# Computing the w_mod product in four column groups of TensorE, from a buffer ring of its own, inside the delta rule

## The reference, cut to what matters

```python
# first block (D_MODEL 1024, SEQ 256)
h = h + gated_deltanet(rmsnorm(h, a_norm), ...)        # qkv, z, chunked delta rule, w_out
h = h + conv_ffn(rmsnorm(h, f_norm[0]), ...)           # up, conv, silu*val, down
kv = rmsnorm(h, kv_norm) @ w_kv
h = h + chunk_attention(rmsnorm(h, b_norm), ...)       # 16 heads, band of 576 keys
h = h + conv_ffn(rmsnorm(h, f_norm[1]), ...)
# second block
mod   = silu(c)     @ w_mod + b_mod                    # 1024 -> 6144, one row
mod_c = silu(c_ctx) @ w_mod + b_mod                    # and one for the context
sh1, sc1, g1, sh2, sc2, g2 = split(mod, 6)
hc = rmsnorm(ctx, norm1) * (1 + csc1) + csh1           # context rows
h  = rmsnorm(x, norm1)   * (1 + sc1)  + sh1
x  = x + g1 * (concat(retention, attention)(h @ w_in, hc @ w_in) @ w_out)
x  = x + g2 * (square(relu((rmsnorm(x, norm2) * (1 + sc2) + sh2) @ w_ff1)) @ w_ff2)
out = rmsnorm(x, final_norm)
```

## Time and profile before

| | before |
|---|---|
| device time, 3 runs | 1300.94, 1303.83, 1306.04 us (median 1303.83) |
| profiled execution: first to last instruction (span) | 1310.7 us |
| profiled execution: mean granted TensorE clock | 0.958 |
| PE busy | 1216.3 us (93% of the span) |
| PEld busy | 1065.0 us (81%) |
| DVE busy | 803.3 us (61%) |
| ACT busy | 567.6 us (43%) |
| POOL busy | 28.4 us (2%) |
| chain that ended last | PE 69%, issue 16%, DVE 9%, ACT 4%, DMA 2% |
| moved by DMA | 192.51 MB, 147 GB/s |

### The profile page before, as it was taken

The page is one execution under the profiler, slowest core; times in us unless marked ns, Lnnn a source line. Parts: engine busy times, 40 slices in busy tenths (PEclk is TensorE's granted clock), DMA queues, the critical chain, the costliest instruction groups (busy, mean ns, idle before and its releaser), DMA issues.

```text
span 1310.7 us, 22039 instructions
## 1 busy us (share of the span) xinstructions
PE 1216.3 (93%) x8276; PEld 1065.0 (81%) x8276; DVE 803.3 (61%) x1352; ACT 567.6 (43%) x918; POOL 28.4 (2%) x27
## 2 busy tenths in 40 slices
PE   4999999999999999898799999999999688999995
PEld 4997769847899988796578999885999456999884
DVE  4994565454588875444446888754456866455654
ACT  5554410023455454445445545544435445344552
POOL 0001000000000000000010000000100000000000
PEclk9997989899999999999799999999999899899998
DMA  7662420054666566555174566665433106466661
GB/s 200 161 187 71 153 72 1 17 177 138 192 185 189 179 208 194 150 176 173 49 257 129 173 179 192 206 194 178 129 97 97 33 1 198 117 184 191 204 194 51
DMA packets 226688, 192.51 MB, mean 147 GB/s; under 512 B 6784, under 2 KB 202496, under 8 KB 226368
## 3 DMA queue, kind: packets, MB, share of 16 engines
q1 hardware_dynamic: 223984, 184.67, 47.2%
q0 software_dynamic: 1456, 6.82, 1.4%
q10 hardware_dynamic: 1184, 0.14, 0.1%
HBM read 190.56 MB, written 1.05 MB: 146 GB/s over the span
## 4 chain that ended last, share of the span: by engine, by line
PE 69%; issue 16%; DVE 9%; ACT 4%; DMA 2%; POOL 1%; SPq 0%; DVEq 0%; POOLq 0%; ACTq 0%
PE ps L565 18%; PE ps L567 17%; PE ps L566 17%; PE ps L443 4%; PE ps L766 3%; PE ps L764 2%; DVE wL L1551 2%; PE ps L774 1%; PE ps L660 1%; DMA raw<-in_w_mod 1%; DMA raw<-in_a_w_in 1%; DVE st_p L1956 1%; ACT xH L1147 1%; ACT wH L1057 1%; PE ps L836 1%
## 5 line engine op out<-in xcount | busy, mean ns | idle before, releaser
L1551 DVE TENSOR_TENSOR wL<-raw,wH 128x1024 fp32r<-128x1024 f32 x298 | 354.7, 1222 | 185.4 <-ACT wH L1057 184.4
L565 PE MATMUL ps<-xH,wH 128*128 128x256 f32 x1216 | 348.2, 286 | 0.0
L566 PE MATMUL ps<-xL,wH 128*128 128x256 f32 x1216 | 347.3, 286 | 0.0
L567 PE MATMUL ps<-xH,wL 128*128 128x256 f32 x1216 | 347.1, 285 | 0.0
L1057 ACT ACTIVATE wH<-raw 128x1024 fp32r<-128x1024 f32 x298 | 302.1, 1053 | 95.1 <-PE ps L567 93.7
L565 PEld LDWEIGHTS ps<-xH,wH 128*128 128x128 f32 x1216 | 236.8, 195 | 2.3 <-issue 2.1
L566 PEld LDWEIGHTS ps<-xL,wH 128*128 128x128 f32 x1216 | 236.8, 195 | 0.0
L567 PEld LDWEIGHTS ps<-xH,wL 128*128 128x128 f32 x1216 | 236.7, 195 | 0.0
L565 PE MATMUL ps<-wH,xH 128*128 128x256 f32 x496 | 144.1, 291 | 3.7 <-DVE xL L1551 3.7
L1095 ACT ACTIVATE stage<-ps 128x512 f32<-128x512 f32 x84 | 50.2, 597 | 222.4 <-PE ps L567 222.4
L566 PE MATMUL ps<-wL,xH 128*128 128x256 f32 x496 | 142.7, 288 | 0.0
(11 more groups left out here) (333 smaller groups left out, 1444.4 us busy)
## 6 DMA issues: line engine op xcount, KB each, us to landing
raw<-in_f_w_up SPq DMA_DIRECT2D x88, 512.0 KB, 4.7
raw<-in_w_ff SPq DMA_DIRECT2D x64, 512.0 KB, 4.2
raw<-in_w_mod SPq DMA_DIRECT2D x48, 512.0 KB, 4.2
raw<-in_f_w_down SPq DMA_DIRECT2D x44, 512.0 KB, 4.3
raw<-in_a_w_in SPq DMA_DIRECT2D x32, 512.0 KB, 4.7
raw<-in_w_in SPq DMA_DIRECT2D x22, 512.0 KB, 4.6
raw<-in_w_kv SPq DMA_DIRECT2D x16, 512.0 KB, 4.6
raw<-in_a_w_out SPq DMA_DIRECT2D x8, 512.0 KB, 4.5
```

The costliest lines, as they stand in the source:

```text
L565: mm(o, l[0], r[0], start=first, stop=False, skip_group_check=check)
L566: mm(o, l[0], r[1], start=False, stop=False, skip_group_check=check)
L567: return mm(o, l[1], r[0], start=False, stop=last, skip_group_check=check)
L1551: return tt(o, x, hi.bitcast(F32), ALU.subtract)
```

## The change

The product runs with another shape and other buffers, and most of it at another place.

**Shape.** `cact` is now 32 columns wide, its columns 2 to 31 zeroed by POOL. A unit is four matmuls of 32 stationary and 256 moving columns, one for each row half k and column half x, and each writes to its own 32 PSUM partitions, 32 * (2k + x). So they lie in four column groups of the PE array. The two row halves are no longer summed by PSUM; the finish does it. `mrow` is 128 x 256, and the finish multiplies it by selection constants: `sel` (four matmuls against 2 columns, L454 of the changed kernel) or `selb` (two matmuls of 256 columns, L458). The constants grow by 260 columns of fp32 for each partition.

**Ring.** The units have a ring of three buffers, `modw`, loaded by POOL's queue in program order between POOL's inverse roots. The `raw` ring on SP carries only layer weights again.

**Place.** Forty units, ten chunks, are in the front of the delta rule and the delta rule itself: 8 among the z blocks, 8 among `products`, 16 in the doubling (the dictionary `fill`: 1 or 2 units after a step, -1 for a finish), 8 in the scan. One chunk stays around the norm f0 and one around kv. None is left in the band attention or around f1, n1 and n2.

```diff
-MOD_PLACES = (("wo_a", 5), ("up0", 1), ("k", 1), ("wo_b", 1), ("up1", 1), ("win", 2), ("ff1", 1))
+MOD_CHUNKS = 12
+MOD_RAW = 3
+MOD_AFTER = {"up0": 11, "k": 12}
-        cact = sb("cact", [P, KD, 2])
-        mrow = sb("mrow", [2, 2, 512])
+        cact = sb("cact", [P, KD, 32])
+        mrow = sb("mrow", [P, 2, 256])
+            modw = sb("modw", [P, MOD_RAW, 2, 512], where=s)
 # ModulationSteps.units
-                    self.pe.wait_ge(mod_in[self.m % RAW], 16 * (self.m // RAW + 1))
+                    self.pe.wait_ge(mod_in[self.m % MOD_RAW], 16 * (self.m // MOD_RAW + 1))
                     for k in range(2):
-                        last = nc.tensor.matmul(mod_bank(h)[0:2, :], cact[:, 2 * u + k],
-                                                raw[:, (U(name) + self.m) % RAW, k * 512:(k + 1) * 512],
-                                                start=u == 0 and k == 0, stop=u == 3 and k == 1)
+                        for x in range(2):
+                            q = 32 * (2 * k + x)
+                            last = nc.tensor.matmul(mod_bank(h)[q:q + 32, 0:256], cact[:, 2 * u + k],
+                                                    modw[:, self.m % MOD_RAW, k, x * 256:(x + 1) * 256],
+                                                    start=u == 0, stop=u == 3)
 # ModulationSteps.finish
-                        last = nc.tensor.matmul(mod_bank(h)[:, 2 * k:2 * k + 2], mrow[:, h % 2, k * P:(k + 1) * P],
-                                                ident[0:2, 0:2], start=True, stop=True)
+                        last = nc.tensor.matmul(mod_bank(h)[:, 2 * k:2 * k + 2], mrow[:, h % 2, (k % 2) * P:(k % 2 + 1) * P],
+                                                K_["sel"][:, 2 * (k // 2):2 * (k // 2) + 2], start=True, stop=True)
 # delta_front_pe
                 sums()
                 z(0)
+                mod.units(3)
                 square_sums()
...
                 z(1)
+                mod.units(1)
...
                 z(2)
+                mod.units(2)
...
                 z(3)
+                mod.units(2)
 # delta_pe
-                mod.units(4)
+                mod.finish()
+                mod.finish()
...
                 products(0)
+                mod.units(2)
                 for g in range(1, 4):
                     products(g)
                     turn_m(g - 1)
+                    mod.units(2)
                 turn_m(3)
-                mod.units(4)
+                fill = {(0, 0): -1, (0, 1): -1, (0, 2): 1, (1, 0): 1, (1, 1): 1, (1, 2): 1, (2, 0): 1, (2, 1): 1, (2, 2): 1,
+                        (3, 0): 1, (3, 1): -1, (3, 2): -1, (4, 0): 2, (4, 1): 2, (4, 2): 2, (5, 0): 2}
...
+                        if fill.get((l, step), 0) < 0:
+                            mod.finish()
+                        mod.units(max(fill.get((l, step), 0), 0))
...
                 heads(4, lambda n: AT[:, 8 + n], lambda n: P_[:, 8 + n])
-                mod.units(4)
                 mod.finish()
                 mod.finish()
-                mod.units(4)
 # band_pe
                 scores(0)
                 scores(1)
-                mod.units(4)
-                mod.finish()
 # program of PE
             token_major("wo_b", X)
-            mod.units(3)
             turn_rows("f1")
-            mod.units(1)
-            mod.finish()
...
-            mod.units(7)
             turn_rows("n1")
-            mod.units(1)
-            mod.finish()
-            mod.finish()
...
-            mod.units(3)
             turn_rows("n2")
-            mod.units(1)
-            mod.finish()
 # POOL
+            def mod_load(first, end):
+                for m in range(first, end):
+                    if m >= MOD_RAW:
+                        pool.wait_ge(mod_used, m - MOD_RAW + 1)
+                    ...
+                    pool.dma_start(modw[:, m % MOD_RAW], src).then_inc(mod_in[m % MOD_RAW], 16)
             norm("a")
+            pool.wait_ge(unit_done, 12)
+            mod_load(0, 6)
...
+            mod_load(6, 42)
...
+            mod_load(42, 43)
             norm("f0")
+            mod_load(43, 47)
...
             norm("kv")
+            mod_load(47, 48)
```

More of the change, by code:

```diff
@@ L331, in build @@
         cond_ready = sem("cond_ready")
-        mod_in = [sem(f"mod_in{i}") for i in range(RAW)]
+        mod_in = [sem(f"mod_in{i}") for i in range(MOD_RAW)]
         mod_used = sem("mod_used")
@@ L989, in _ @@
             pe.wait_ge(y_ready, 4)
-            pe.wait_ge(mod_act, sum(MOD_AT["wo_a"]))
+            pe.wait_ge(mod_act, 10)
             token_major("wo_a", X)
@@ L1244, in delta_act @@
                     cp(MT[:, 4 * g:4 * g + 4].rearrange("p a b -> p (a b)"), ps[2 + g % 2][:]).then_inc(mt_act, 1)
-                mod_keep()
-                mod_keep()
+                for _ in range(3):
+                    mod_keep()
+                    mod_keep()
+                    mod_place()
+                    mod_place()
                 def banks(first, bank, o):
```

108 lines of the change are left out of this document (38 added, 70 removed).

## The result

The changed kernel takes 1318.81 us (median; 1316.76 to 1320.81), the kernel before 1302.38 on the same chip: ratio 1.0133, 95% interval 1.0103 to 1.0162. So 16 us slower, where 3 us faster was forecast, and outside the range of 1288 to 1316.

What follows compares the result with a forecast made beforehand. The prediction took PE (93% busy) as the bound, but only where the stage waits for it. Its terms summed to -3.2 us, 1307.5 against the profiled span 1310.7, corrected to 1301 for the timed runs; range 1288 to 1316.

Steps and rivals of the forecast that it cites:

- The term for the larger constants: Before the first matmul: 0.13 MB of constants at 222 GB/s takes 0.6 us, counted as +0.5.
- the doubling's term: Doubling in the delta rule: 16 units 9.3 us, four finishes 4.2, +13.5; wrong above 20 or below 8.
- the base: Whole kernel: sum -3.2 on the profiled span 1310.7, then about 7 us off because timed runs lie lower.
- The price of a unit: Each unit of the product: 0.43 us with four column groups together, 0.86 at half clock; 1.81 before.
- The charge for entering: Entering and leaving the four-group form: 0.2 us a call (0 to 0.5).
- C: Only two column groups stream at once: unit 0.9 us, 30 units on the path, +12, 1313; chance 0.13.
- E: Groups run one after another: unit stays at 1.8 us, +42 less some 8, about 1335; chance 0.05.
- D: The ring starves: at 7 us a load +15, 1316; decides from about 5.5 us a load; chance 0.10.
- The front: Delta rule's front: units ahead of the column sums and among the z blocks, total +4.0 us (1 to 6).
- The set-up: Ahead of the doubling: eight units between products and turns, -4.8 us if hidden, 0 if not; half taken, -2.4.
- Scan and tail: Delta rule's scan +0.4 us together; tail, colder PE at y's transposes and first wo_a tiles, +1.2 (0 to 3).
- The norms: First matmuls of the layers behind the norms: f0 -2.8 us, kv +0.6, f1 -4.6, n1 -1.0, n2 -3.6.

Runs made afterwards that it cites:

- warm_setup: after_aligned plus four fp32 matmuls of 2 by 512 columns, result unread, in PE's gap ahead of the doubling; 1304.0 us, ratio 1.0027.
- before, second: The kernel before, profiled again with no edit; ratio 1.0001, span 1302.8 us.
- after_aligned: The changed kernel with 32 bytes of padding behind the constants, aH back at its old address; 1307.69 us, ratio 1.0049.
- after_x: The changed kernel with 32 bytes of padding ahead of xH and no other padding; 1297.37 us, ratio 0.9953.
- warm_tail: after_aligned plus sixteen fp32 matmuls of 2 by 512 columns, result unread, under DVE's closing work of the delta rule; 1304.47 us, ratio 1.0020.
- late8: after_aligned with the doubling's last eight units moved to the scan, the scan's eight under DVE's closing work with extra warming matmuls; 1303.97 us, ratio 1.0008.
- place_only: The changed kernel with the old unit shape (2 columns by 512) and the constants, cact and mrow of the kernel before; 1356.02 us, ratio 1.0397.
- finish_early: after_aligned with the finishes of chunks 2 and 3 ahead of the doubling's first step; 1302.18 us, ratio 1.0011.
- no_fill: The changed kernel without chunks 4 to 7: their 16 doubling units, loads, two finishes in the doubling and two in the scan; 1298.68 us, ratio 0.9976.
- spread: after_aligned with 12 of the doubling's 16 units moved: into the scan, under DVE's closing work, one chunk into the band attention; 1298.08 us, ratio 0.9980.
- shape_x: The kernel before with only the unit's shape changed, plus 32 bytes of padding ahead of xH; 1278.25 us, ratio 0.9821.

## Why the prediction was wrong

Two steps failed. The term for the larger constants, +0.5, held their DMA alone and put what they do to the addresses behind them at nothing, without a reason; that was 11 us, 6 of them countable. And the doubling's term, +13.5, had the units and the finishes but no clock; the doubling grew by 21.7, beyond the 20 from which the forecast had called itself wrong. A third error was in the base, and hid in the choice of the profile. The terms one by one:

**The price of a unit** was right: 0.43 for the second of a pair, and 0.57 alone with 0.17 more in the step behind it, 0.74 in all, against a forecast of 0.43 and 0.2. In the timeline four records of a unit start within 0.02 us and the other four 0.22 to 0.24 us later. An estimate from the speedup for three column tiles that the Trainium skill gives (TensorE: Matmul & The Clock Gate, Measured speedup vs the span model) would be 0.55; the trace has four groups at 0.43. The charge for entering, which the Trainium skill's rule on draining (TensorEngine Tiling (Array Packing), Key Properties) had put in doubt, is 0.14 for the unit and 0.17 for the step behind it, and the second of these the old shape pays as well. Rivals C and E are out, and D too: the loads took 4.5 us in the median, below the 5.5 from which D decides.

**The front** was sized wrongly by 4 us in the change's favour. I had priced three units at half clock. They ran at full clock, 1.50 us in all, and the 64 column sums behind them took 10.23 instead of 13.67 (13.58 in the earlier trace rows), because the clock fell at 109 us and not at 102. The forecast had taken 1 us off for this and not 3.4.

**The set-up** came out at -1.1 instead of -2.4: the doubling starts 6.9 earlier and the finishes 0.1 later, which makes -7.0, of which the finishes are 1.68 - 7.55 = -5.9. The ring of three was the brake, as written: two loads, of 4.28 and 5.41 us, stand in the chain there.

**The doubling** is the step that failed in the delta rule: +21.7 against +13.5. Its own terms add up to 8 x 0.74 + 5.1 for the four pairs + 3.5 for the finishes = 14.5, near the 13.5. The other 7 are the clock: 6.27 - 3.77 for the first step, which starts cold, and 2.9 + 0.4 + 1.6 for the second fall. I had written that the old units ahead of the doubling cost 9.25 us and could go. They had also done their slow first half at low clock while DVE was not ready yet, and the doubling then ran from its start at a clock of 1.00. I read that clock and didn't ask what had brought it about. With four matmuls for nobody in that gap (warm_setup) the first step is back at 3.77 us.

**Scan and tail**: +2.2 against +0.4 for the scan. The cold transposes of y are 3.0 us longer on the chain (3.69 against 0.67) where the tail had 1.2, but the units ahead of f0 are shorter, and from DVE's closing work to f0's scaling it is 1.0 in all.

**The norms** came nearly as forecast, if measured from the profile that they were read from. From the start of DVE's scaling (xn) to the first matmul of the next layer, in us:

| norm | before, first | before, second | after | against the first | forecast |
|---|---|---|---|---|---|
| f0 | 11.1 | 9.5 | 8.1 | -2.9 | -2.8 |
| kv | 6.7 | 6.7 | 8.2 | +1.5 | +0.6 |
| f1 | 10.9 | 9.1 | 6.0 | -4.9 | -4.6 |
| n1 | 9.1 | 9.2 | 8.1 | -1.0 | -1.0 |
| n2 | 11.2 | 11.4 | 8.2 | -3.1 | -3.6 |

Here is the error in the base. The first profile was 8 us longer than the second, and 3.4 of these lie at f0 and f1 (11.1 and 10.9 instead of 9.5 and 9.1). The forecast took some 7 us off for the long profile, and then counted the whole distances at f0 and f1 as they stood in it, so that the 3.4 went in twice. Against the second profile f0 and f1 gave 4.5 and not 7.4.

The other parts of the table by stages lie between the norms. The slower matmuls of down are 1.7 us in each of the first two feed-forward layers and 2.5 in ff2; the rest of the first of these layers is 1.3 longer. The band gave 4.0 (forecast 3.3). The second block's attention, ahead of n2, was 2.0 longer, where nothing was forecast and after_aligned shows 0.4.

Where the product no longer stands ahead of the turning, the turning itself runs cold:

```profile
1113.70 3.67 PE L610 MATMUL ps<-cst,xn 128*128 128x128 f32 x16 [6.25 <-DVE xn L1560]
```

was 1.97 in the earlier trace rows. At kv the turning took 3.67 us and the finish 2.08, instead of 1.97 and 1.05, at a clock of 0.50; the shorter unit between them gave 0.8 of these back, and the distance grew by 1.5. For f0 the last unit's load stands in the chain, 5.84 us from its issue, which is the forecast's 4.8 and its 1 for POOL:

```profile
340.42 5.84 DMA modw<-in_w_mod
...
346.31 0.68 PE ps L441 x8
...
347.45 1.73 PE ps L458 x4
```

The Trainium skill's trap in SBUF — State Buffer, SBUF: two separate sides (a GpSimd DMA whose descriptors wait for DVE) would explain a us there, over the median of 4.5; but it would bear on the load at kv as well, which is issued at 546.04 us beside the same scaling of xn and landed in 4.3 (the DMA issues between 546 and 552 us):

```profile
modw<-in_w_mod POOLq DMA_DIRECT2D x1, 512.0 KB, 4.3
```

So this case doesn't show such a wait. What differs is the traffic: 323 GB/s moved between 340 and 347 us, 89 GB/s between 546 and 552.

**What was in no term**: the addresses. 11 us of the 16 went when 32 bytes were added (1.0133 to 1.0049), 6.0 of them countable as 912 matmuls by 6.6 ns. The other 5 are not shown to be the address: in the two profiles 4.4 us of the difference stand in the scan (31.9 us long against 27.5), where the clock was at 1.2 GHz for 14 us in one and for 7 in the other. The constants appeared in my sum as 0.13 MB of DMA. They were also 1040 bytes in each partition ahead of every later tensor. Without this loss the change stands at 1.0049 (1.0016 to 1.0082), half a per cent slower and inside the forecast's range.

**The place** still decides the sign. On the old address of aH the shape alone stands at 0.9939 and the whole change at 1.0049, so the new places and the ring cost 1.1%, 14 us. The forecast never made that comparison: its sum took shape and place together.

**Still open.** Why the clock falls a second time with PE busy throughout. In seven profiles (after, after_aligned, after_x, warm_setup, warm_tail, late8, place_only) it falls in the same place, the third step, 11 to 14 us after the start of the doubling and behind the two finishes. It doesn't in finish_early, where the finishes stand ahead of the doubling, nor in any of the ten profiles with the old order, which have no finish there. But no_fill and spread have the finishes in that place, and no fall. So the finishes are in every case with the fall, and are not enough for it. And it is open what relation of addresses gives which cadence: four offsets of aH were measured (0 good; -32, +32, +64 bad) and two of xH (+32 better than 0).

## What to carry to other kernels

After a change of any buffer's size, compare the distance between matmuls of stages that the change doesn't touch, at full clock: if it differs, the addresses moved, and 32 bytes of padding are a change to be tried by themselves (here worth 8 to 21 us, as much as the order of the work). When a profile is longer than the timed runs, profile once more before gains are read from its waits. Before filler work is taken from in front of a PE-bound stretch, read at which clock it ran, and count the cold start of what follows it. A stretch in which PE never waits sells no room: each insertion there costs its full length and a little more.

## What the runs showed of the hardware

- Four fp32 matmuls of 128 rows by 32 columns with 256 moving columns each, into four groups of 32 PSUM partitions, run at once: four records start within 0.02 us, and the eight records of a unit took 0.43 us behind another unit, the time of two that follow each other in one group (0.226 each).
- At full clock, matmuls with 512 moving columns came every 226.7 or 233.3 ns and those with 256 every 120 or 117 ns (118.3 where the moved operand was the stationary one), depending on where the fp32r operands start in SBUF. Each followed its own tensor, and both good values could be had together (shape_x).
- Full-width fp32 matmuls lost 0.17 us in the step behind a unit with 2 or 32 stationary columns, and nothing behind a finish with 128.
- Runs of one kernel differ by up to 22 us (after_x, 1287 to 1309), and profiles of one kernel place the falls of the clock differently, so that two profiles don't show a difference of a few us between kernels; the ratios do.
